# Turning the experts' gathered rows with VectorE and transfers within SBUF instead of TensorE

## What is computed

```python
def ec_moe(h, router_w, w_gate, w_up, w_down):
    cap = 2 * t // 16                       # 128 tokens for each of 16 experts
    aff = softmax(h @ router_w)
    gate, idx = lax.top_k(jnp.swapaxes(aff, 1, 2), cap)
    xs = h[bidx, idx]                       # (16, 128, 1024)
    hid = silu(xs @ w_gate) * (xs @ w_up)   # w_gate, w_up: 1024 x 512 per expert
    ye = (hid @ w_down) * gate[..., None]   # w_down: 512 x 1024 per expert
    return jnp.zeros_like(h).at[bidx, idx].add(ye)
```

## Time and profile before

| | us |
|---|---|
| median of 3 runs (1385.27 to 1390.42) | 1387.87 |
| profiled execution, its own time | 1388.71 |
| span from its first to its last instruction | 1387.0 |
| PE busy (90% of the span) | 1245.3 |
| DVE busy (55%) | 764.1 |
| ACT busy (31%) | 430.8 |
| POOL busy (16%) | 220.3 |

### The profile page before, as it was taken

The page is one execution under the profiler, slowest core; times in us unless marked ns, Lnnn a source line. Parts: engine busy times, 40 slices in busy tenths (PEclk is TensorE's granted clock), DMA queues, the critical chain, the costliest instruction groups (busy, mean ns, idle before and its releaser), DMA issues.

```text
span 1387.0 us, 14619 instructions
## 1 busy us (share of the span) xinstructions
PE 1245.3 (90%) x5410; PEld 733.2 (53%) x5410; DVE 764.1 (55%) x1110; ACT 430.8 (31%) x1094; POOL 220.3 (16%) x206
## 2 busy tenths in 40 slices
PE   4999999999999998899999689992199999999983
PEld 3455555455455555889999345552044444444441
DVE  5199889887927776598887446546601101010124
ACT  6233232313111114677786243432011010110122
POOL 0300000010000031266665000000101011010112
PEclk9899999999999999999999799995599999999996
DMA  9823454552052451567676724426479999999967
GB/s 365 265 77 98 125 157 139 158 164 92 17 167 50 106 110 29 149 180 218 206 211 207 260 91 182 181 77 245 149 273 318 350 330 340 333 330 349 320 226 161
DMA packets 207532, 270.69 MB, mean 195 GB/s; under 512 B 75053, under 2 KB 124198, under 8 KB 207462
## 3 DMA queue, kind: packets, MB, share of 16 engines
q1 hardware_dynamic: 187118, 210.97, 46.8%
q0 software_dynamic: 14272, 52.43, 12.6%
q10 hardware_dynamic: 6072, 6.35, 1.3%
HBM read 217.75 MB, written 51.97 MB: 194 GB/s over the span
## 4 chain that ended last, share of the span: by engine, by line
PE 66%; DVE 13%; DMA 10%; ACT 4%; issue 3%; SPq 3%; POOL 0%; POOLq 0%; ACTq 0%; DVEq 0%
PE ps L1874 23%; PE ps L1115 13%; PE ps L411 7%; PE ps L1134 6%; DVE arena L2241 3%; PE ps L1078 2%; DMA y_dram<-arena 2%; DMA arena<-zt_dram 2%; DMA tok_dram<-arena 2%; DMA arena<-ada_w 2%; PE ps L1773 1%; PE ps L495 1%; PE ps L468 1%; PE ps L469 1%; PE ps L1104 1%
## 5 line engine op out<-in xcount | busy, mean ns | idle before, releaser
L1874 PE MATMUL ps<-arena 128*128 128x512 f32 (+1 forms) x1072 | 423.4, 552 | 0.0
L1874 PEld LDWEIGHTS ps<-arena 128*128 128x128 f32 x1072 | 201.3, 190 | 199.5 <-issue 194.4
L1115 PE MATMUL ps<-arena 128*128 128x512 f32 x512 | 226.8, 596 | 1.4 <-ACT arena L1238 1.4
L2241 DVE SCALAR_TENSOR_TENSOR arena<-arena,taps 128x1024 f32<-128x1024 f32 x160 | 209.3, 1308 | 5.5
L1115 PEld LDWEIGHTS ps<-arena 128*128 128x128 f32 x512 | 96.5, 191 | 116.8 <-issue 114.8
L411 PE MATMUL ps<-arena 128*128 128x128 f32 x1080 | 132.2, 277 | 9.7 <-DVE arena L630 4.2
L411 PEld LDWEIGHTS ps<-arena 128*128 128x128 f32 x1080 | 127.2, 192 | 15.8 <-DVE arena L630 5.2
L1401 DVE TENSOR_TENSOR arena<-arena,ps 128x512 f32<-128x512 f32 x16 | 11.0, 688 | 224.1 <-PE ps L1115 224.1
L1078 PE MATMUL ps<-arena 128*128 128x512 f32 x256 | 116.0, 608 | 4.2 <-ACT arena L1187 4.2
L1134 PE MATMUL ps<-arena 128*128 128x512 f32 x256 | 112.8, 593 | 0.0
L1078 PEld LDWEIGHTS ps<-arena 128*128 128x128 f32 x256 | 48.6, 194 | 62.3 <-issue 56.2
(11 more groups left out here) (314 smaller groups left out, 1536.1 us busy)
## 6 DMA issues: line engine op xcount, KB each, us to landing
arena<-exp_w_gate SPq DMA_DIRECT2D x16, 2048.0 KB, 11.0
arena<-exp_w_up SPq DMA_DIRECT2D x16, 2048.0 KB, 9.1
arena<-exp_w_down SPq DMA_DIRECT2D x16, 2048.0 KB, 11.2
arena<-ada_w POOLq DMA_DIRECT2D x16, 1024.0 KB, 6.6
arena<-w_in SPq DMA_DIRECT2D x28, 512.0 KB, 4.7
arena<-ada_w SPq DMA_DIRECT2D x4, 2048.0 KB, 19.9
arena<-x SPq DMA_DIRECT2D x16, 512.0 KB, 6.6
arena<-g_dram SPq DMA_DIRECT2D x16, 512.0 KB, 6.2
```

Of the source, the lines that this page charges most:

```text
L1115: last = mm(ps[gu_bank[s] + j][:], xsT[s][:, k, :], ew[s][j][:, k, :], start=(k == 0), stop=(k == KD - 1))
L1874: last = mm(ps[3 * (m % 2) + gi][:, 0:w], wring[(m + 1) % NW][:, k, :], hT[:, k, o:o + w], start=(k == 0), stop=(k == KD - 1))
L2241: ins = v.scalar_tensor_tensor(accg, cin_l[ci % 2][:, j // 3:j // 3 + GR, j % 3:j % 3 + GW], tp[:, j:j + 1], accg, ALU.mult, ALU.add)
```

## The change

The gathered rows are no longer turned by TensorE. VectorE transposes them in blocks of 32 by 32 into a new tile `xt` (two buffers), writing each block's elements 8 apart. Then SyncE moves 16 pieces of 32 partitions by 256 elements (32 KB each, runs of 1 KB) from `xt` to the partitions where they belong in `xsT`. This puts feature 256 r + 32 k + i on partition 32 r + i for each k, so the gate and up weights are loaded in that order too, in four pieces of 32 partitions each instead of one DMA; the runs stay 2 KB long. TensorE reads `xsT` with a step of 8 elements. The transposes on TensorE and the copies on ScalarE go away. In SyncE's order the moves of expert e+1 stand ahead of its weights and wait until up(e-1) is done. GpSimd's gathers now wait for VectorE's transpose to have read the rows. The order of down, scatter and tail is as it was.

```diff
+        xt = [take(D) for _ in range(2)]
...
-        xsT = [take(D).rearrange("p (k n) -> p k n", k=KD) for _ in range(2)]
+        xsT = [take(D) for _ in range(2)]
...
-        wg_e = exp_w_gate.rearrange("a e (k p) n -> (a e) p k n", p=P)
-        wu_e = exp_w_up.rearrange("a e (k p) n -> (a e) p k n", p=P)
+        wg_e = exp_w_gate.rearrange("a e (r k i) n -> (a e) r i k n", r=NB, i=BL)
+        wu_e = exp_w_up.rearrange("a e (r k i) n -> (a e) r i k n", r=NB, i=BL)
...
-                    sp_.dma_start(ew[s][j], src[e]).then_inc(sem(f"gu_in{s}"), 16)
+                    for r in range(NB):
+                        sp_.dma_start(ew[s][j][r * BL:(r + 1) * BL], src[e, r]).then_inc(sem(f"gu_in{s}"), 16)
...
+            def turned_in(e):
+
+                sp_.wait_ge(sem("xsps"), e + 1)
+                if e >= 2:
+                    sp_.wait_ge(sem("gu"), 2 * (e - 1))
+                for b in range(NB):
+                    for r in range(NB):
+                        sp_.dma_start(xsT[e % 2][r * BL:(r + 1) * BL, b * 256:(b + 1) * 256],
+                                      xt[e % 2][b * BL:(b + 1) * BL, r * 256:(r + 1) * 256]).then_inc(sem(f"xsT{e % 2}"), 16)
...
                 if e == 0:
                     sp_.wait_ge(sem("logit"), NL)
                     sp_.wait_ge(sem("y_zero"), 32 * NL)
+                    load_in(1)
+                    load_down(0)
+                    turned_in(0)
+                    turned_in(1)
+                    continue
                 if e + 1 < E_N:
+                    turned_in(e + 1)
                     load_in(e + 1)
...
-            def xs_half(e, h):
...
-                    pe.wait_ge(sem("xsT"), 2 * e + 2)
-                    pe.wait_ge(sem(f"gu_in{s}"), 32 * (e // 2 + 1))
+                    pe.wait_ge(sem(f"xsT{s}"), 16 * NB * NB * (e // 2 + 1))
+                    pe.wait_ge(sem(f"gu_in{s}"), 32 * NB * (e // 2 + 1))
...
-                    last = mm(ps[gu_bank[s] + j][:], xsT[s][:, k, :], ew[s][j][:, k, :], start=(k == 0), stop=(k == KD - 1))
+                    turned = xsT[s][:, k::KD]
+                    last = mm(ps[gu_bank[s] + j][:], turned, ew[s][j][:, k, :], start=(k == 0), stop=(k == KD - 1))
...
-            def xs_copy(e, h):
...
+            def rows_turned(e):
+                dve.wait_ge(sem(f"xs_in{e % NX}"), 16 * (e // NX + 1))
+                if e >= 2:
+                    dve.wait_ge(sem(f"xsT{e % 2}"), 16 * NB * NB * (e // 2))
+                v.transpose(xt[e % 2].rearrange("p (r j k) -> p r k j", r=NB, k=KD),
+                            xs[e % NX].rearrange("p (r k j) -> p r k j", r=NB, k=KD)).then_inc(sem("xsps"), 1)
+
+            rows_turned(0)
+            rows_turned(1)
             for e in range(E_N + 1):
                 if e < E_N:
...
+                if e + 2 < E_N:
+                    rows_turned(e + 2)
...
-                pool.wait_ge(sem("xsps"), 2 * (E_N - NX + k + 1))
+                pool.wait_ge(sem("xsps"), E_N - NX + k + 1)
...
-                    pool.wait_ge(sem("xsps"), 2 * e)
+                    pool.wait_ge(sem("xsps"), e)
```

More of the change, by code:

```diff
@@ L1136, in down @@
                 last.then_inc(sem("down"), 1)
-            xs_half(0, 0)
-            xs_half(0, 1)
             for e in range(-1, E_N):
@@ L1142, in pe_tail @@
                     gate_up(e + 1, 0)
-                if e + 2 < E_N:
-                    xs_half(e + 2, 0)
                 if e >= 0:
@@ L1154, in pe_tail @@
                     gate_up(e + 1, 1)
-                if e + 2 < E_N:
-                    xs_half(e + 2, 1)
                 if e >= 0:
@@ L1248, in tile_root @@
                 root_of(t, yt[:, t, :])
-            xs_copy(0, 0)
-            xs_copy(0, 1)
             for e in range(E_N + 1):
@@ L1258, in act_tail @@
                     a(hid[e % 2], ps[gu_bank[e % 2]][:], ACT.Silu).then_inc(sem("sg"), 1)
-                if e + 1 < E_N:
-                    xs_copy(e + 1, 0)
                 if e >= 1:
@@ L1263, in act_tail @@
                     a(hidT[(e - 1) % 2], heads(ps[1][:]), ACT.Copy).then_inc(sem("hidT"), 1)
-                if e + 1 < E_N:
-                    xs_copy(e + 1, 1)
             for t in range(N_FIRST, NL):
```

## The result

The changed kernel takes 1565.84 us (median of four runs, 1563.53 to 1583.2) against 1388.76 for the kernel before (four runs, 1385.27 to 1390.42). The ratio is 1.130, with a 95% interval from 1.126 to 1.134: 177 us slower. The prediction was slower too, but at 1471 us, and its range ended at 1515. The profiled execution took 1565.08 us, its span is 1563.3.

A forecast was written before the change was run, and what follows sets the result against it. PE was taken to set the pace at 21.92 us per expert, the DMA a hair behind. With the DMA at 28 us per expert, 1388.7 + 82.6 - 0.8 gave 1471 us, range 1396 to 1515.

The forecast's parts named there:

- the rate of 32 partitions: Gate and up pieces and moves on 32 partitions run at 238 GB/s, so gate and up take 17.6 us per expert.
- the overlap: Gather and scatter, 4.0 us per expert, may run beside held-back pieces: 29.7 us without overlap, 25.7 with all, 28 taken.
- The start: Before the periods: first gate at 1009.6, 6.6 us late; gate and up weights of expert 2 start at 1032.1.
- the tail: After gate(14): same length as before; gate(15) another 6 us late, absorbed by room of 9.5 us of y transfers.
- W: The DMA work of one expert: 21.3 us before the change, taken as 28 us after it.
- The term of the moves itself: The 16 transfers within SBUF add 0.52 MB per expert on the DMA, 2.2 us at 238 GB/s.
- the prediction's sign of a dear transpose or issue: At the start: gate(0) later than 1012 would mean the block transpose or the issue is dearer than taken.
- upper bound for the strided weight load: On PE: a load four times as long, 0.76 us, adds 10.6 us per expert, a period of 31.6; nothing taken.
- A: Expert stage: pieces held back on 32 partitions slow the DMA; 1471 us, 1443 to 1510, chance 0.59.
- Rival B: Weight loads: only bytes count, pieces move as fast as whole loads; W 22.7 us, time 1401 us, chance 0.26.
- rival C: Expert stage: PE still sets the pace and the transfers slip in; 1380.5 us, 1377 to 1392, chance 0.10.
- The rate of 182: A load of 128 KB into 32 partitions; at its bare rate in GB/s, W is 35.8 us, time about 1570.

The follow-up runs named there:

- e2: The kernel before with only gate and up weights loaded in four pieces of 32 partitions, old order of features: 1501.96 us, ratio 1.079.
- m1: A kernel that only moves data, the weight matrices cut in several ways one after the other, nothing of the layer computed: one execution, 340.97 us.
- e8: The changed kernel without its 16 moves per expert, pieces of 32 partitions kept, rows in the wrong place: 1522.16 us, ratio 1.094.
- e3: The kernel before with gate and up weights loaded in four pieces each, every piece over all 128 partitions: 1388.54 us, ratio 0.999.
- e1: The changed kernel with whole gate and up loads over 128 partitions, the transpose's write order altered to suit, moves kept: 1409.56 us, ratio 1.014.
- e4: e1 without its 16 moves per expert, TensorE reading the unmoved tile, so numbers are wrong: 1376.71 us, ratio 0.991.
- e10: e2 with ScalarE issuing the pieces of partitions 64 to 127 when SyncE issues those of 0 to 63: 1454.96 us, ratio 1.043.
- e7: The kernel before with only the turned rows laid out in steps of 8 elements, as the change reads them: 1392.98 us, ratio 1.002.

## Why the prediction failed

The profiled executions leave 93.7 us between span and forecast (1563.3 - 1469.6; the second is the span before, 1387.0, and the 82.6 us forecast). The mechanism was right; its largest term, the rate of 32 partitions, was mis-sized, and three smaller steps failed beside it. The rate makes 35 of the 93.7 us (2.7 in each of 12 periods and once before gate(2)), the overlap 20, the rest of the start 13, the tail 14, and 12 stay unexplained. With the rate alone put right the forecast would have been some 1506 us, still 60 short.

**The rate of 32 partitions** is the step that failed: "I take 238 GB/s for everything on 32 partitions, since two of three rows are near it." Measured are 209 GB/s in the change, 204 in e2, 219 in m1, all below the 222 on which the range's upper end was built. The row of 238 is one microsecond long and follows on a store of 512 KB on all partitions, and the row of 222 is 0.7 us long. In stretches of ten and more microseconds the number is lower. With 207 (between the change's 209 and e2's 204) gate and up take 20.3 us instead of 17.6, 2.7 more per expert. The load of 128 KB at 182 GB/s and a share of 0.58 was left open: m1 lands such a load in 2.4 us, and a lone piece of 512 KB on 32 partitions still moves at 328 and 348 GB/s from 321.30 to 321.90 us. So one piece by itself is no measure of the rate of a run of pieces.

The Trainium skill, page "SBUF — State Buffer", section "Door 1: The DMA port swizzle", has 32 and 64 adjacent partitions reach the same half of the DMA ports, with an asymptote of 218 GB/s. The runs of pieces of 32 and of 64 partitions at 219 and 215 GB/s in m1 agree with both. By it the prediction had estimated 19.2 us for the weights, nearer to the 20.3 than the term that the sum used.

**The overlap.** W was taken as 28, as the gather and scatter "may run beside the held-back pieces". The sum without overlap was 29.7, and with the lower rate 29.7 + 2.7 = 32.4; the period was 33.4. So no overlap is to be seen: the forecast's 1.7 us per expert were not there. The two terms make 4.4 us per expert and 1.0 stays unexplained; together they are 400.6 - 12 x 28 = 64.6 us over the 12 periods. For e2, which has no moves, the same sum would be 32.4 - 2.2 = 30.2, and its period is 31.6. The term of the moves itself, 2.2 us, was nearly right: 2.0 in e8.

**The start.** The transpose and the issues were dearer than taken. In the groups by source line, beside the earlier trace rows (ns least, median, most):

```profile
L1392 DVE STREAM_TRANSPOSE arena<-arena x16: 2015/2031/2034, 999.7 to 1455.8; 128x1024 f32<-128x1024 f32 x16
...
L1021 SPq DMA_DIRECT2D arena<-arena x256: 507/591/4687, 1001.7 to 1468.2; - x128
```

2.03 us for the transpose, not 1.2, and 591 ns for a move's issue, not 432. Gate(0) came at 1013.14 (forecast 1009.6, and the prediction's sign of a dear transpose or issue was a gate(0) later than 1012). The timeline shows what matters more:

```profile
1001.70 39.82 SPq L1021 DMA_DIRECT2D arena<-arena  x48
```

Three sets of 16 moves until 1041.52, and only then the weights of expert 2, where 1032.1 was forecast and 1011.77 was the time before. The third set starts only at 1031.51, because of a wait that the forecast left out: it needs VectorE's transpose of expert 2's rows, which stands in VectorE's program behind the product of expert 0.

```profile
1028.84 0.69 DVE L1402 TENSOR_TENSOR arena<-arena,ps 128x512 f32<-128x512 f32 x1 [25.26 <-PE ps L1125]
1029.44 2.03 DVE L1392 STREAM_TRANSPOSE arena<-arena 128x1024 f32<-128x1024 f32 x1
```

Meanwhile the DMA was nearly idle:

```profile
1013.00:1040.00 27.00, 26.86 (x62) 18.70 (x63) 2.64 (x2) 1.68 (x3) 0.00 (x0) 0.94 0.13 34
```

The share is 0.13 for 27 us. The later issue (1041.52, forecast 1032.1) is 9.4 us of the miss: 3.5 from the later gate(0), 2.8 from product and transpose, 3.1 from issues that took 10.0 us and not 6.9. From there to gate(2) the forecast had 17.6 + 2.1 = 19.7 us, and it took 25.7 (1067.22 - 1041.52), 6.0 more: 2.7 of it is the rate again, and SyncE had put the down weights and the next moves into the same queue; what these cost was not tested. Gate(2) is 15.4 us late, and with the 64.6 of the periods gate(14) is 80.0 late (1467.82, forecast 1387.8).

**The tail.** "the path there runs over the y tiles and their 9.5 us of transfers, and has that much room." From gate(14) to the end it took 95.5 us where it had been 81.8. The first two rows are of the kernel before, the others of the change:

```profile
1341.53 0.69 DVE L1401 TENSOR_TENSOR arena<-arena,ps 128x512 f32<-128x512 f32 x1 [12.83 <-PE ps L1115]
1345.99 0.16 DVE L1390 RECIPROCAL rstd<-rstd 128x1 f32<-128x1 f32 x1 [3.78 <-ACT rstd L1244]
...
1504.86 9.04 SPq L1041 DMA_DIRECT2D arena<-y_dram  x8
...
1523.24 0.69 DVE L1402 TENSOR_TENSOR arena<-arena,ps 128x512 f32<-128x512 f32 x1 [29.62 <-PE ps L1125]
1523.85 0.16 DVE L1382 RECIPROCAL rstd<-rstd 128x1 f32<-128x1 f32 x1
1524.04 1.29 DVE L1383 SCALAR_TENSOR_TENSOR arena<-arena,rstd 128x1024 f32<-128x1024 f32 x1
```

DVE's scaling of the y tiles (L1383, before L1391) stands in its program behind the product of expert 15 (L1402, before L1401). In the kernel before DVE idles for 3.78 us between the two, until the y tiles are read and squared: that is the room, not 9.5 us. And gate(15) came 38.1 us after gate(14) (1505.92 - 1467.82) where it had been 21.9, 16 us more and not the 6 forecast, as it waited 13.75 us. The product comes 55.4 us after gate(14) instead of 36.4, and now nothing is left to wait for behind it: 19.1 - 3.8 = 15.3 us, of which the end gives 1.6 back. 80.0 + 13.7 = 93.7.

One reading in the prediction was wrong without an effect: its upper bound for the strided weight load, a period of 31.6 us, is above and not below the upper end of A, 31.2.

What was right: the mechanism (A), the side, a DMA share of 1 with a falling rate (forecast roughly 280 GB/s, measured 243), a wait ahead of every gate (forecast 7 us; from gate(3) to gate(14) 4.9 to 16.2, 9.8 in the mean), PE's strided read at almost nothing (0.12 us per up, inside the bounds), the removed transposes at no gain while the DMA sets the pace, and that SP is no bound of its own once the stage runs (read from the DMA share of 1.07, not tested alone). Rival B falls with e2 and e3 (same bytes, 112 us apart); rival C falls with e1 and e4 (PE's gain needs moves that cost nothing). The rate of 182 had been priced at 1570 us and left outside the range; that the time came near it is luck, as the rate was not 182: the lost overlap, the start and the tail made up for it.

By the runs the 177 us are: pieces by partition 112 (e2 against the kernel before), the weights' later start at expert 2 with the rest of the reordering 18 to 20 (e8 against e2), the moves 44 to 47 (the change against e8). The two ranges come from taking the medians as they are or each against the kernel before of its group.

**What stays open.** Why two queues give 371 GB/s alone and 289 beside the gathers and the rest of the kernel. Whether it is the opposite halves or only the second queue that gives the gain in e10 and m1: no run put two queues on the same half. Whether gather and scatter can overlap with held-back pieces at all. No version that computes the layer beats the kernel before: e4, which leaves the moves out, shows that taking the eight transposes off PE is worth 0.9% with moves that cost nothing, and no run tried a way to bring the rows to their partitions without the DMA queues.

## What to carry to other kernels

Cut a load along the free dimension and not by partition: four pieces over 128 partitions cost nothing, four of 32 cost 8% here. When a new order of features seems to ask for other weights, look first whether the order in which the transpose writes can absorb it, as in e1. Here PE was full and the DMA at 0.99, and work taken from one and given to the other was lost work (e1, 1.4% slower). Read a rate from ten or more microseconds in which nothing else is under way: the rows of one microsecond and less gave 238 and 222 GB/s, the long ones 204 to 219. And when one engine's work moves to another, look at what stands ahead of it in that engine's program: here the third transpose, and the moves and weights after it, stood behind the product of expert 0.

## What the runs showed of the hardware

- A full DMA share says nothing of the rate: from one queue 389 GB/s on 128 partitions, 215 to 224 on 32 or 64 adjacent ones, all at 1.05 to 1.07 (m1, one execution).
- Two queues that fill opposite halves at once: 371 GB/s in m1. The Trainium skill, page "DMA: Bandwidth & Descriptors", section "Rules for kernel authors", says that two transfers to disjoint halves serialize, from one issuing engine or two. From one queue the runs agree (224 against 219 by reordering); from two they differ, 371 in m1, and about 50 us gained in e10. The measurement decides.
- A stationary operand (float32, 128x128) with a step of 8 elements loads in 314 ns instead of 190, nearly all hidden under matmuls of 430 (e7, ratio 1.002).
- A block transpose that scatters its output takes 2.03 us for 128x1024 (the change), where 128x1280 took 1.51 in the kernel before.
- Small moves within SBUF (32 KB) issue in 0.59 us each at the median of the change and 0.64 in m1, where the DMA engines stand at a share of 0.20; in the full queue of the change one took up to 4.7 us.
